# Splitting half of the last weight piece of each expert unit on GpSimd

## What is computed

```
def run_block(args):                       # a block of tokens of one expert e
    xblk, e = args
    hu = xblk @ w1[e] + b1[e]              # 1024 -> 2048
    x_glu = jnp.minimum(hu[:, :D_FF], SWIGLU_LIMIT)
    x_lin = jnp.clip(hu[:, D_FF:], -SWIGLU_LIMIT, SWIGLU_LIMIT)
    act = x_glu * jax.nn.sigmoid(SWIGLU_ALPHA * x_glu) * (x_lin + 1.0)
    return act @ w2[e] + b2[e]             # 1024 -> 1024
...
y = zeros.at[row_tok].add(yb * row_gate)   # weighted sum back into the tokens
```

## Time and profile before

| | us |
|---|---|
| median of 3 runs | 2738.23 (2736.86 to 2741.65) |
| span of the profiled execution | 2736.2 |
| experts in it, about | 870 to 2736 |
| PE busy | 2587.9 (95%) |
| DVE busy | 2045.3 (75%) |
| ACT busy | 1453.7 (53%) |
| POOL busy | 539.6 (20%) |

### The profile page before, as it was taken

How to read it: one execution, slowest core, us unless ns; L and a number is a source line. 1 busy time by engine, 2 the same in 40 slices (tenths; PEclk the granted TensorE clock), 3 DMA queues, 4 the chain that set the end, 5 groups by cost and what they waited for, 6 DMA issues and landing times.

```text
span 2736.2 us, 46067 instructions
## 1 busy us (share of the span) xinstructions
PE 2587.9 (95%) x16405; PEld 2212.7 (81%) x16406; DVE 2045.3 (75%) x2500; ACT 1453.7 (53%) x1639; POOL 539.6 (20%) x423
## 2 busy tenths in 40 slices
PE   7998987999896999999999999999999999999995
PEld 3896866777885888777887979899989897898885
DVE  5447888545765987999879787866686778978786
ACT  5446565214443765777557465544454546645554
POOL 0035565200023112121212111110121112111111
PEclk9999998999998999999999999999999999999998
DMA  7121011442333996999879697866586779968783
GB/s 289 39 88 44 22 42 57 173 152 93 109 92 127 386 364 229 365 360 359 287 260 362 235 313 258 283 208 209 190 301 206 247 249 314 344 209 296 261 309 133
DMA packets 274722, 606.26 MB, mean 222 GB/s; under 512 B 21788, under 2 KB 52932, under 8 KB 273520
## 3 DMA queue, kind: packets, MB, share of 16 engines
q1 hardware_dynamic: 254256, 561.62, 57.1%
q0 software_dynamic: 20384, 43.51, 6.9%
HBM read 582.09 MB, written 46.97 MB: 230 GB/s over the span
## 4 chain that ended last, share of the span: by engine, by line
PE 40%; issue 10%; DVE 8%; ACT 4%; DMA 4%; DVEq 1%; POOL 1%; ACTq 0%; POOLq 0%
PE e_acc L2488 7%; PE e_acc L2491 7%; PE e_acc L2489 7%; PE e_acc L2461 5%; PE e_acc L2463 5%; PE e_acc L2462 5%; DMA list_now<-lists 3%; DVE e_slot_r L2646 3%; ACT whi L2574 3%; PE e_tb L2430 1%; DVE yo L2733 1%; DVE e_glu L2709 1%; PE e_acc L2523 1%; DVE e_xlo L2655 1%; POOL sum L2388 1%
## 5 line engine op out<-in xcount | busy, mean ns | idle before, releaser
L2574 ACT ACTIVATE whi<-e_slot 128x2048 fp32r<-128x2048 f32 x296 | 561.0, 1913 | 393.7 <-PE e_acc L2491 327.0
L2646 DVE TENSOR_TENSOR e_slot_r<-e_slot,whi 128x2048 fp32r<-128x2048 f32 x296 | 674.6, 2286 | 106.3 <-ACT whi L2574 106.3
L2488 PE MATMUL e_acc<-e_xhi,whi 128*128 128x256 f32 x1664 | 398.8, 282 | 3.3 <-ACT e_xhi L2578 3.3
L2574 ACT ACTIVATE whi<-slot 128x2048 fp32r<-128x2048 f32 x148 | 283.2, 1913 | 192.4 <-PE e_acc L2463 192.4
L2646 DVE TENSOR_TENSOR slot_r<-slot,whi 128x2048 fp32r<-128x2048 f32 x151 | 344.7, 2285 | 18.1 <-ACT whi L2574 16.5
L2461 PE MATMUL e_acc<-whi,e_ahi 128*128 128x512 f32 x800 | 319.4, 399 | 0.0
L2488 PEld LDWEIGHTS e_acc<-e_xhi,whi 128*128 128x128 f32 x1664 | 313.1, 188 | 6.3 <-ACT e_xhi L2578 6.3
L2463 PE MATMUL e_acc<-whi,e_alo 128*128 128x512 f32 x800 | 313.4, 392 | 0.0
L2462 PE MATMUL e_acc<-e_slot_r,e_ahi 128*128 128x512 f32 x800 | 311.5, 389 | 0.0
L2388 POOL DMA_INDIRECT sum<-yo,e_idx_now x48 | 117.8, 2454 | 973.3 <-issue 518.9
L2461 PE MATMUL e_acc<-whi,e_xhi 128*128 128x512 f32 x768 | 303.6, 395 | 1.8 <-DVE e_slot_r L2646 1.6
(11 more groups left out here) (432 smaller groups left out, 5014.9 us busy)
## 6 DMA issues: line engine op xcount, KB each, us to landing
e_slot<-in_w SPq DMA_DIRECT2D x296, 1024.0 KB, 7.1
slot<-in_w SPq DMA_DIRECT2D x151, 1024.0 KB, 6.4
rv<-in_w_ada SPq DMA_DIRECT2D x32, 512.0 KB, 5.6
slot<-in_w_in SPq DMA_DIRECT2D x9, 1024.0 KB, 9.6
wa<-in_w_ada SPq DMA_DIRECT2D x8, 1024.0 KB, 17.1
slot<-in_w_in SPq DMA_DIRECT2D x12, 512.0 KB, 4.2
xt<-in_x SPq DMA_DIRECT2D x8, 512.0 KB, 14.7
slot<-in_w_out SPq DMA_DIRECT2D x4, 1024.0 KB, 13.9
```

What stands on the lines that cost most here:

```text
L2488: pe.matmul(out[:, c, :], whi[i % RING][:, w], xhi[:, kk, :], start=first, stop=False, skip_group_check=True)
L2574: act.activation(whi[i % RING][:], raw[i % PIECES][:], ACT.Copy).then_inc(S["whi_made"], 1)
L2646: v.tensor_tensor(wlo[i % PIECES][:], raw[i % PIECES][:], whi[i % RING][:].bitcast(F32), ALU.subtract).then_inc(S["wlo_made"], 1)
```

## The change

In `rest`, DVE subtracts only the first 1024 of the 2048 columns of piece 11 (`HEAD`). A new function `tail(u)` on POOL subtracts the other 1024 (`TAIL`) once ACT has made `whi` of that piece. It stands on POOL behind the gathers and ahead of the scatter, and for the last unit behind the loop ahead of `last_sum`. PE waits for both halves before `down(11)`.

```
+        LAST = PIECES - 1
+        HEAD, TAIL = slice(0, WSLOT // 2), slice(WSLOT // 2, WSLOT)
...
+            def tail(u):
+                g.wait_ge(S["whi_made"], u * PIECES + PIECES)
+                alone(g, S["g_passed"])
+                g.tensor_tensor(wlo[LAST][:, TAIL], raw[LAST][:, TAIL], whi[LAST % RING][:, TAIL].bitcast(F32), ALU.subtract).then_inc(S["tail_made"], 1)
...
                 for b in range(NB):
                     gather(b)
 
+                tail(u)
                 cnt = count_of(g, u)
...
             rows_free(before_last)
+            tail(before_last)
             g.wait_ge(S["scattered"], before_last * (16 * NB))
...
                         pe.wait_ge(S["wlo_made"], u * PIECES + (i + 1))
+                        if i == LAST:
+                            pe.wait_ge(S["tail_made"], u + 1)
...
             def rest(i, u):
                 v.wait_ge(S["whi_made"], u * PIECES + (i + 1))
-                v.tensor_tensor(wlo[i % PIECES][:], raw[i % PIECES][:], whi[i % RING][:].bitcast(F32), ALU.subtract).then_inc(S["wlo_made"], 1)
+                part = HEAD if i == LAST else slice(0, WSLOT)
+                v.tensor_tensor(wlo[i % PIECES][:, part], raw[i % PIECES][:, part], whi[i % RING][:, part].bitcast(F32), ALU.subtract).then_inc(S["wlo_made"], 1)
```

More of the change, by code:

```diff
@@ L2252, in experts @@
         tb = [t.ps(f"e_tb{i}") for i in range(2)]
-        names = """const_in set bcol_ready mid_ready next_ready now_ready pick_ready gates_ready whi_made wlo_made
+        names = """tail_made const_in set bcol_ready mid_ready next_ready now_ready pick_ready gates_ready whi_made wlo_made
         piece_done glu_ready lin_ready mix_ready sig_made act_ready turned hi_made lo_made y_taken scattered
```

## The result

| | before | after |
|---|---|---|
| median of 20 runs, us | 2736.94 (2732.03 to 2741.65) | 2741.45 (2736.12 to 2747.18) |
| ratio after / before | | 1.0014, 95% interval 1.0008 to 1.0020 |
| span of the profiled execution, us | 2736.2 | 2735.9 |

The account below looks back on a forecast made before the run. PE bounds double units; in single units PE and DVE are equally full. Span 2736.2 + 6.2 (single units) + 1.5 (last unit) = 2743.9 us, with the median 2.0 above: 2745.9 us; range 2733 to 2760 us.

Parts of the forecast that it names:

- DVE and POOL exclude each other when DVE reads two tiles in SBUF: In single units, POOL passes behind `rest(10)` until 1250.92, holding the half `rest(11)` to 1252.01 instead of 1251.75.
- +0.26 us in each single unit, 24 times, +6.2 us: In single units, DVE and PE's next start come 0.26 us later, 24 times: +6.2 us.
- Double units 0: In the 13 double units, POOL delays the second `e_lin` product and `rest(10)`, covered by DVE's idle time: 0.
- The last unit +1.5 us: At the kernel's end, the first `last_sum` gather, behind `tail`, lands 0.3 to 1.9 us after PE wants it: +1.5 us.
- the term is 0: In the last unit, the gather may land sooner with fewer transfers beside it, adding 0.
- The rival of the saving coming through, 11.3 us faster: In single units, no exclusion: DVE 1.06 us earlier, PE wins 11.3 us in all, 2726.9 us; chance 0.12.
- the 0.68 us of its two stops: In single units, PE's winnable waits for DVE: 0.5 us for `e_lin` and 0.18 us for `xlo`.
- The rival "It cancels", 2738 to 2743 us: In single units, POOL's half is held less long or PE's stop hides more: 2738 to 2743 us; chance 0.14.
- Forecast 7.7 us slower: For the whole kernel, a median of 2745.9 us, 7.7 us or 0.28% slower.

Follow-up runs that it names:

- e1: The changed kernel without POOL's subtraction and PE's wait for it, DVE still subtracting only half of piece 11: 15.9 us faster than the kernel before.
- e2: The changed kernel with DVE subtracting all of piece 11 and POOL doing a subtraction into an unread tile: 18.9 us slower than the kernel before.
- e5: The changed kernel run again, with no further edit: 4.9 us slower than the kernel before.
- e4: The changed kernel with piece 10 shared between DVE and POOL instead of piece 11: 25.7 us slower than the kernel before.
- e6: The kernel before run again, unchanged, for a second trace: -1.6 us (-4.4 to +1.1).

## Why the prediction came out as it did

- *DVE and POOL exclude each other when DVE reads two tiles in SBUF.* Right, shown by e1 and e2 on the same instruction (1.22 and 2.53 us), and placed right: POOL behind `rest(10)`, `alo` free, `rest(11)` held. POOL's end, 2.26 us behind `rest(10)`, and the held end of `rest(11)` came to 0.01 us as worked out from the mixer's rows.
- *+0.26 us in each single unit, 24 times, +6.2 us.* Right for a unit in the steady stretch (37.55 against 37.29), and 23 of the 24 places show it: 23 halves of 2.52 or 2.53 us, and 23 waits of PE for `xlo`, 0.25 us longer each. Unit 0 was put in with the others and is not like them: DVE stood idle there for 1.45 us before `alo`, the half wasn't held (1.29 us), and 0.98 us came back. By these terms the units cost 23 x 0.26 - 0.98 = 5.0 us; the traces average +4.3 from there on. The nine units behind a double one wait for a list at their middle, and their lengths scatter by as much as the effect; whether some of the 0.26 us is absorbed there, the two traces of each kernel don't settle.
- *Double units 0.* Right: within 0.08 us. The product of `e_lin` before `rest(10)` was stretched by 2.09 us and covered, as put.
- *The last unit +1.5 us.* **Wrong**: it was 0. POOL was let through in the gap, as assumed. But the landing time of 6.3 to 7.9 us was that of gathers issued while weights were coming in (the DMA engines 98% busy); at 37% it was 4.7 us (5.1 in e5, at 40%), and the gather landed 1.7 us before it was wanted. In e4, at 71%, it was 6.8 us, and in e6, before again, with the DMA engines fully busy, 5.4 and 6.9. So traffic is a likely cause and not a shown one; no run changed it alone. The text named that case ("the term is 0") and didn't take it. In the table of waits of the last unit PE doesn't appear.
- *The rival of the saving coming through, 11.3 us faster.* It didn't come to be, but e1 shows its price: 15.9 us. Two terms were off in opposite directions: a single unit behind a single one shrinks by 1.00 us, not by the 0.68 us of its two stops, and the ten entries into double units give little. The 0.32 us are there in the starts of PE's products. A stop costs PE more than the idle time before it, since the products behind it follow later too. At `e_lin`, before and in e1:

```profile
1235.67 0.40 PE L2463 MATMUL e_acc<-whi,e_xlo 128*128 128x512 f32 x1
1236.59 0.66 PE L2430 MATMUL e_tb<-ident,e_lin 128*128 128x128 f32 x4 [0.52 <-DVE e_lin L2728]
```

```profile
1232.48 0.40 PE L2470 MATMUL e_acc<-whi,e_xlo 128*128 128x512 f32 x1
1232.72 0.60 PE L2437 MATMUL e_tb<-ident,e_lin 128*128 128x128 f32 x4
```

  The step from one start to the next was 0.92 us and is 0.24: 0.68 us, not 0.5, and 0.06 more behind the transposes. At `xlo` the two steps around the unit's first product (1255.39, 1255.80, 1256.14 before; 1251.46, 1251.69, 1251.92 in e1) fell from 0.75 to 0.46 us: 0.29, not 0.18. Together 1.03 us.
- *The rival "It cancels", 2738 to 2743 us.* The measured median lies in its band, but what it asks for (POOL through sooner, or PE's stop hiding more) happened in unit 0 alone; in 23 units the cost was there in full.
- *Forecast 7.7 us slower, measured 3.8 (2.2 to 5.5) and 4.9 (2.5 to 7.4).* 1.5 us of the difference is the last unit and 1.2 us is unit 0 (0.26 that wasn't paid and 0.98 given back). That leaves 5.0 us, which lies within both intervals. The right direction rested on one reading: that the half costs DVE more than the half it gives away.

## What to carry to other kernels

Work handed from VectorE to GpSimd is not off VectorE's path if both read SBUF (the memory of the tiles; PSUM is the one that PE writes to) and VectorE reads two tiles there: price it as GpSimd's full length, less what VectorE does meanwhile with PSUM operands or while idle. Size the part to that cover (here 410 columns, not 1024) and place it there; the same half cost 4 to 5 us at piece 11 and 26 us one piece earlier, and a smaller split in two covered places gained 10 us. And before a row's latency is used elsewhere, look at what ran beside it: the gathers that landed in 6.3 to 7.9 us with the DMA engines 98% busy took 4.7 us where they were 37% busy.

## What was not expected of the hardware

- In the last unit a waiting POOL operation got in where DVE's next two-input operation was only 0.04 us away (2686.62 to 2686.66), one that waits for its forerunner's result (3.31 us for 1.22). In the mixer it had stayed out over three DVE operations that follow each other without a gap; the first two stand ahead of those in the earlier trace rows, and POOL asked at 283.57:

```profile
283.29 0.41 DVE L1210 TENSOR_TENSOR h_wk<-h_wk,h_keyA 128x256 f32<-128x256 f32 x1
283.62 0.42 DVE L1211 TENSOR_TENSOR h_wk<-h_wk,h_keyA 128x256 f32<-128x256 f32 x1
```

  That the gap decides is argued from these places; no run changed it. That the first to issue goes first, as the Trainium skill says (SBUF — State Buffer, Who interferes with whom), is what e4 and the last unit show; the three operations remain an exception to it.
- POOL's subtraction of 128 x 1024 took 2.26 us behind its release when it wrote fp32r from two tiles, and 1.75 us with one tile as both inputs and a bf16 output. For 320, 416 and 1024 columns it took 0.74, 0.96 and 2.26 us.
- The same 0.25 us of VectorE counts 23 times as a cost and some 14 times as a gain: at the entries into double units PE, once it doesn't stop for `xlo`, stops longer for `xhi`.
